# First tap of the values' convolution moved to ScalarE, with the order of two taps, one cast and one silu changed

## The reference

```python
c = xp[:, 0:L] * conv_w[0]                    # first tap of a causal convolution of width 4
for i in range(1, CONV_W):
    c = c + xp[:, i:i + L] * conv_w[i]        # three more taps
c = jax.nn.silu(c)
q, k, v = jnp.split(c, ...)                   # each of q, k, v has its own convolution
...
lower = jnp.where(strict, einsum(kb, k) * decay, 0.0)
sol = triangular_solve(eye + lower, rhs)      # per chunk
...
o = rmsnorm(tr(o), norm_w) * jax.nn.silu(z)
```

## Time and profile before

| | us |
|---|---|
| median of three runs | 3575.13 |
| the profiled execution, its own time | 3572.24 |
| its span | 3570.2 |
| PE busy in the span | 3441.2 (96%) |
| DVE busy | 2033.6 (57%) |
| ACT busy | 1491.5 (42%) |
| POOL busy | 774.6 (22%) |

### The profile page before, as it was taken

One profiled execution on the slowest core, in us unless ns is written; L12 is line 12 of the kernel. 1 busy time (PEld: TensorE's weight loads), 2 busy tenths in 40 slices (PEclk: granted clock), 3 DMA queues, 4 the chain that ended last, 5 costly groups with the idle time before them and its releaser, 6 DMA issues. The chain is left out here.

```text
span 3570.2 us, 65011 instructions
## 1 busy us (share of the span) xinstructions
PE 3441.2 (96%) x25088; PEld 3274.5 (92%) x25088; DVE 2033.6 (57%) x3415; ACT 1491.5 (42%) x3083; POOL 774.6 (22%) x621
## 2 busy tenths in 40 slices
PE   7999999999999999999999999998999999999998
PEld 7999999988988888777999999997999899999998
DVE  7655556745555555543666666667332675556555
ACT  5222235645454455433444444444322632223444
POOL 3332301102121221000333223334000233231000
PEclk9999999999999999999999999999899999999999
DMA  4222246721221123695011111012332323223654
GB/s 159 82 81 76 86 147 212 230 90 52 66 66 61 61 70 118 207 369 188 21 43 37 43 43 37 26 30 80 128 90 77 116 75 87 72 81 118 218 192 140
DMA packets 343926, 372.72 MB, mean 104 GB/s; under 512 B 20980, under 2 KB 252222, under 8 KB 343502
## 3 DMA queue, kind: packets, MB, share of 16 engines
q1 hardware_dynamic: 334694, 339.49, 30.3%
q0 software_dynamic: 8880, 29.21, 2.3%
q10 hardware_dynamic: 84, 0.35, 0.0%
HBM read 297.42 MB, written 71.55 MB: 103 GB/s over the span
## 5 line engine op out<-in xcount | busy, mean ns | idle before, releaser
L657 PE MATMUL ps<-p_hi,w_hi 128*128 128x352 f32 x912 | 304.7, 334 | 3.9 <-PEq L120 1.5
L657 PE MATMUL ps<-p_hi,w_lo 128*128 128x352 f32 x912 | 293.7, 322 | 0.0
L657 PE MATMUL ps<-p_lo,w_hi 128*128 128x352 f32 x912 | 293.3, 322 | 0.0
L1930 PE MATMUL ps<-p_hi,w_hi 128*128 128x352 f32 x768 | 257.6, 335 | 0.0
L1930 PE MATMUL ps<-p_hi,w_lo 128*128 128x352 f32 x768 | 253.7, 330 | 0.0
L1930 PE MATMUL ps<-p_lo,w_hi 128*128 128x352 f32 x768 | 253.0, 329 | 0.0
L1866 POOL TENSOR_TENSOR dl_mk<-dl_lo_t,cst 128x512 f32<-128x512 f32 x112 | 172.2, 1552 | 71.7 <-PE ps L2083 38.9
L657 PEld LDWEIGHTS ps<-p_hi,w_hi 128*128 128x128 f32 x912 | 172.5, 189 | 6.3 <-issue 3.7
L2776 PE MATMUL ps<-op_hid_hi,w_hi 128*128 128x384 f32 (+1 forms) x528 | 170.8, 323 | 4.0 <-DVE w_lo L2451 2.2
L2776 PE MATMUL ps<-f_hid_hi,w_hi 128*128 128x352 f32 x528 | 171.9, 326 | 1.9 <-DVE w_lo L2451 1.9
L657 PEld LDWEIGHTS ps<-p_lo,w_hi 128*128 128x128 f32 x912 | 172.5, 189 | 0.0
(11 more groups left out here) (675 smaller groups left out, 10945.9 us busy)
## 6 DMA issues: line engine op xcount, KB each, us to landing
w_raw<-in_ffn_w_out_dram SPq DMA_DIRECT2D x136, 256.0 KB, 3.3
w_raw<-in_w_in_dram SPq DMA_DIRECT2D x67, 512.0 KB, 3.9
sa_v<-in_cache_v_dram SPq DMA_DIRECT2D x120, 256.0 KB, 6.6
w_raw<-in_ffn_w_in_dram SPq DMA_DIRECT2D x48, 512.0 KB, 5.2
sa_k<-in_cache_k_dram SPq DMA_DIRECT2D x72, 256.0 KB, 5.3
f_s<-in_ffn_w_out_dram SPq DMA_DIRECT2D x64, 256.0 KB, 3.1
pair_s<-in_ffn_w_out_dram SPq DMA_DIRECT2D x64, 256.0 KB, 3.2
d_hid<-f_gb SPq DMA_DIRECT2D x44, 264.0 KB, 2.2
```

The costliest lines, as they stand in the source:

```text
L657: mm = nc.tensor.matmul(m.ps[:, bank, 0:CH], a[:, k, w], b[:, f, cols(c)], start=(f == 0 and i == 0), stop=(f == KT - 1 and i == 2))
L1930: mm = nc.tensor.matmul(m.ps[:, (k + c) % 2, 0:CH], a[:, k, f * P:(f + 1) * P], x[:, f, cols(c)], start=(j == 0), stop=(j == len(terms) - 1))
```

## The change

- ACT makes the first tap of the values' convolution, as an activation Copy with the weight as its scale, behind the exponentials and ahead of z's silus. DVE keeps the write of the old rows (the pad) and does it between `clamps(1)` and `clamps(2)`.
- Taps 1 and 2 stand on DVE ahead of level one, tap 3 in level three; before, tap 1 stood ahead of level one, and taps 2 and 3 in levels two and four.
- ACT's cast behind z's last silu goes behind level one's two copies.
- ACT's silu of the next head's k, which stood behind the scan's last step, goes into that step, ahead of the copy of its output row and that row's square.

```diff
@@ scalar engine, head(h)
+                act.wait_ge(padded, 3 * h + 4)
+                wait(act, vt_mm, 3 * h)
+                nc.scalar.activation(cs[:, 2, 0:CO], xc[:, 2, 0:CO], ACT.Copy,
+                                     scale=m.convw[:, bass.ds(h + 2 * H, 1), :].rearrange("p o w -> p (o w)")[:, 0:1]).then_inc(conv_done, 1)
                 for c in range(3):
-                    take(h, "z", c)
+                    take(h, "z", c, weights=False)
...
                         moves(2 * (lev - 1) + x, x, P if lev < LAST else P // 2)
+                    if lev == 1:
+                        n, k = unit(h, "z")
+                        if exists(n + 2):
+                            high(n + 2, k)
...
                         take(h, *ends[t])
+                    if more and t == TT - 1:
+                        silus(h + 1, 1)
                     act.wait_ge(o_mm, TT * h + t + 1)
...
-                if more:
-                    silus(h + 1, 1)
@@ vector engine
-                dve.wait_ge(padded, 3 * x + u + 2)
-                nc.vector.tensor_scalar(cs[:, u, 0:CO], xc[:, u, 0:CO], wgt[:, 0:1], None, ALU.mult).then_inc(conv_done, 1)
+                if u < 2:
+                    wgt = ...
+                    dve.wait_ge(padded, 3 * x + u + 2)
+                    nc.vector.tensor_scalar(cs[:, u, 0:CO], xc[:, u, 0:CO], wgt[:, 0:1], None, ALU.mult).then_inc(conv_done, 1)
...
                 for x in range(3):
                     clamps(x)
+                    if x == 1:
+                        gather(h, 2)
...
-                gather(h, 2)
                 product(h, 2, 1)
+                product(h, 2, 2)
...
-                    if lev in (2, 4):
-                        product(h, 2, lev // 2 + 1)
+                    if lev == 3:
+                        product(h, 2, 3)
```

More of the change, by code:

```diff
@@ L1552, in gather @@
                     wait(dve, vt_mm, 3 * x)
-                wgt = m.convw[:, bass.ds(x + u * H, 1), :].rearrange("p o w -> p (o w)")
                 nc.vector.tensor_scalar(sample_cols(xc[:, u, :])[:, :, 0:3], m.cst8[:, bass.ds(x + u * H, 1), :].rearrange("p o (b w) -> p (o b) w", w=3),
                                         1.0, None, ALU.mult).then_inc(padded, 1)
-                dve.wait_ge(padded, 3 * x + u + 2)
-                nc.vector.tensor_scalar(cs[:, u, 0:CO], xc[:, u, 0:CO], wgt[:, 0:1], None, ALU.mult).then_inc(conv_done, 1)
+                if u < 2:
+                    wgt = m.convw[:, bass.ds(x + u * H, 1), :].rearrange("p o w -> p (o w)")
+                    dve.wait_ge(padded, 3 * x + u + 2)
+                    nc.vector.tensor_scalar(cs[:, u, 0:CO], xc[:, u, 0:CO], wgt[:, 0:1], None, ALU.mult).then_inc(conv_done, 1)
             def product(x, u, i):
```

## The result

The changed kernel takes 3564.91 us in the median of 15 runs (3556.83 to 3570.62), the kernel before 3572.18 us in the median of its 15 (3564.53 to 3585.63). The ratio is 0.9967, with a 95% interval of 0.9954 to 0.9980, so it is faster by about 12 us (7 to 16); the two medians lie 7.3 us apart. A second set of runs of the same two kernels gave 0.9964 (0.9949 to 0.9979). The forecast was 3.3 us, no measurable change. The sign was right and the size was not.

A forecast was written before the change was run, and what follows sets the result against it. PE, busy 96% of 3570.2 us, was taken to bound the kernel. Inner heads' - 1.3 us and head 7's - 2.0 us made - 3.3 us, from the median 3575.13 to 3571.8 us; eight-in-ten range 3561 to 3580 us.

The forecast's parts named there:

- head 7's, "- 2.0 us": Head 7's levels: two stalls of 2.49 and 2.76 us become one of about 2.5 us, gaining 2.0 us.
- My bound of -4.5 us: Head 7's levels: the most the change could gain there, if PE finds its work ready each time.
- The inner heads: Seven heads ahead of head 7: waits removed and added in the levels sum to - 0.18 us each, - 1.3 us together.
- The tap on ACT: Ahead of z's silus: 1.1 us, fitting into ACT's 2.10 us wait for z's first projection, at cost 0.
- The turn: Between heads: the silu's move shifts PE's idle 0.57 us from first to third transpose, gain 0.
- rival 1: Level two's masks on POOL come as early as before; 13 us gained in all, 3562 us; chance 12%.
- rival 2: ACT gains 0.6 us at each turn between heads, 4.2 us more in seven turns, 3567.6 us; chance 8%.
- rival 4: Ahead of level two, POOL's kd runs before tap 1 and PE starts 0.45 us late; 3574 us; chance 6%.
- rival 3: A slow clock behind the scan's first step spreads from two inner heads to all seven; 3580 us; chance 14%.

The follow-up runs named there:

- experiment 5: Changed kernel with POOL's kd moved from ahead of level two's masks to between level zero's two masks; ratio 0.9949 to the kernel before.
- experiment 2: Kernel before, in head 7 alone taps 1 and 2 ahead of level one and tap 3 in level three, first tap still on DVE; ratio 1.0000.
- experiment 4: Changed kernel with the values' first tap back on DVE in all heads; ratio 0.9995 to the kernel before.
- experiment 3: Kernel before with head 7 alone in the whole changed order, without the silu's move; ratio 0.9966 to the kernel before.
- experiment 1: Changed kernel with head 7's taps 2 and 3 back in levels two and four; ratio 0.9983 to the kernel before.
- experiment 6: As experiment 5, with tap 1 among DVE's products, taps 2 and 3 ahead of level one, none in a level; 3554.65 us, ratio 0.9938.

## Why the prediction was wrong in size

**The term that failed is head 7's, "- 2.0 us".** Its stall part was right: "Two stalls turn into one of about 2.5 us", and they did, 2.49 + 2.76 us into 2.67 + 0.48, 2.10 us less. What failed is the sentence that the slow clock in the wake of such a stall "comes once in either case by this count". In the kernel before it came twice: behind level four's stall, where the first 16 matmuls took 3.33 us instead of 2.05 and the next 16 2.35 instead of 2.00, and again behind level six's, where the tail ran at a clock of 0.70. In the changed kernel it came neither time behind the one stall that was left (2.05 us in both profiles), and the tail's clock was 0.89. With two stalls head 7 ran at a granted clock of 0.81 to 0.86 in each of six profiles, with one at 0.87 to 0.94 in each of seven. In the first pair of profiles the levels from level two's first matmul on took 26.56 us before (52.68 - 26.12) and 22.86 after (46.90 - 24.04): 3.70 us less, of which the stalls are 2.10 and the other 1.60 about what the slow matmuls cost (1.28 + 0.35). So of the pair's 8.18 us my term priced 2.0, near the 2.10 that the stalls measured, and put the slow matmuls, the 2.40 us of the tail and the 2.08 ahead of level two at nothing. By the table's means the levels are worth 52.67 - 48.44 = 4.2 us, and the tail, where the instructions are the same, 34.99 - 32.38 = 2.6 us more; together 6.9 us. I had priced the idle time of a stall and left out that each stall can cost PE twice, once as idle time and once as slow matmuls behind it. My bound of -4.5 us had the same gap.

**The inner heads came as forecast.** An inner head without a slow stretch took 102.46 us before (47.87 + 54.59) and 102.30 after (47.78 + 54.52): - 0.16, forecast - 0.18. The waits stand where the forecast put them: 1.08 us for the mask (forecast 1.0), 0.51 ahead of level five (0.45), none ahead of levels four and six. The split differs a little: 0.07 of the 0.16 us came at the turn, which I had put at 0. The Trainium skill, page "SBUF — State Buffer", section "SBUF: two separate sides", had it that one side waits for the other's whole instruction; the trace agrees, with kd's 1.97 us and the tap's 1.14 us counted from the other's end, and in experiment 5 the tap without kd in front took 1.34. (Where the prediction says that without the lock "the second rival's sum would be nearer", the rival that fits is the first, in which POOL keeps up.)

**The tap on ACT** took 1.19 us, not 1.1, and ACT's wait for z's first projection, 2.10 us before, hid it (1.00 us is left of it). The page "ScalarE: Activation LUTs" of the Trainium skill, section "What ACT_TABLE_LOAD costs", gives a fixed part, a price per column and some 93 ns for each pointer operand; the estimate from it, 280 + 0.833 x 1080 = 1180 ns, is nearer than mine, which scaled a whole row by its columns. What I did not see is what ACT's tap is for: experiments 2 and 4 show that without it the whole gain is lost, because three operations of DVE ahead of level one make a long stall again.

**The turn** was right: the wait moved from the first transpose to the third.

**The rivals.** POOL did not keep up (rival 1) and the turn did not pay (rival 2). kd did not go first (rival 4). The clock (rival 3) is real, but it did not come into all inner heads as that rival feared, and profiles of one kernel differ in it: the slow stretch behind the scan's first step came in two inner heads in both profiles of before, in one and in none of the changed kernel, in two in one profile of experiment 3 and in four in the other, in five in those of experiments 2 and 5. It costs 1.6 or 3.2 us a head.

**What stays open.** Head 7's 6.9 us and the inner heads' 7 x 0.16 = 1.1 us make 8.0 us; the ratio says 12, with an interval that begins at 7.

The timed executions show where to look. Of 106 of the kernel before, 41 took over 3578 us, with a mean of 3582.5; the other 65 have a mean of 3570.0. None of 27 of the changed kernel took over 3570.7, and their mean is 3564.2. Against the shorter executions of before the change is thus worth 5.9 us, and the rest of the 10.7 us between the two means over all executions is that the long ones are gone. Both profiles of the kernel before are of short ones (3572.24 and 3572.27 us). The one profile of a long execution is experiment 2's (3581.28 us): five of its scans have a slow stretch of 3.2 us, and the seven scans with their turns take 396.84 us, 12.5 more than before's 384.38. With one stall in head 7 (the changed kernel, the silu back, experiment 3) 1 of 51 executions took over 3578 us, and with two in experiments 2 and 4 and with the silu alone 11 of 36; but in experiment 1, with two as well, none of 12. Why the change should keep slow stretches out of scans that lie ahead of head 7 is not shown.

Nor do the parts add up: head 7 alone gave 0.9966, all but head 7's taps 0.9983, together more than the whole. The forecast had 1.3 us for what experiment 1 leaves, and its ratio says 6, with an interval from 0.4 to 11. That the stalls shorten or lengthen the tail is not shown either, since experiment 6 had none and the longer tail. Open too is why head 7 reached level two at 24 us in some kernels and at 26 in others.

## What to carry to other kernels

Where PE is over 95% busy, don't price a stall by its idle time alone: read the matmuls behind it, and the granted clock of the stretch that follows, with the stall and without. In one head two stalls of 2.5 us cost 4 us more than one did in the levels and 7 in the whole head (means of six profiles each; the tail's share is not shown to be the stalls'), and the same taps spread over seven heads with waits of 0.5 us gained 0.2 us a head. Before a second operation goes in front of a waiting engine, find another engine for the first; and if DVE and POOL both work there, move POOL's big operation to where DVE waits for somebody else: that was worth 1.5 us a head, more than the whole reordering of the taps.

## What the runs showed of the hardware

A stall of 2.33 us, the same in length and place, was followed by slow matmuls in every second head and by fast ones in the others (experiment 4). One kernel, profiled twice, had two heads with a slow stretch and then four, three of them at 3.2 us. These are windows of one of the three in the second profile of experiment 3; its scan starts at 1866.43:

```profile
1865.00:1870.00 5.00, 5.00 (x39) 4.84 (x37) 2.21 (x4) 0.68 (x3) 1.89 (x1) 0.66 0.37 105
1870.00:1875.00 5.00, 5.00 (x41) 4.56 (x40) 1.40 (x4) 2.09 (x6) 1.26 (x2) 1.00 0.04 10
1875.00:1880.00 5.00, 5.00 (x25) 4.94 (x25) 1.60 (x2) 0.75 (x4) 0.00 (x0) 0.66 0.01 2
1880.00:1885.00 5.00, 5.00 (x37) 4.87 (x36) 3.10 (x5) 1.43 (x6) 0.00 (x0) 1.00 0.00 0
```

PE has no idle time in the four windows, and still the clock is at 0.66 in two of them. A stretch of 3.2 us is two falls of the clock, one as the scan starts, right behind level six's 64x64 matmuls, and one some 10 us later, behind the first step; a stretch of 1.6 us has the later one alone. In the changed kernel's only stretch of 3.2 us PE was busy for 7.09 of the 7.21 us ahead of the scan (2370.00 to 2377.21), and the clock was 0.58 in the next 4 us. Ahead of the later fall stand 16 small matmuls of 8 columns each; that they, or the 64x64 ones, are the cause was not tried.
